# A two-block transformer on one core: in the compression of keys and values the weights become the operand that stays in the array

## The reference, cut to what matters

```python
def nsa_compress(t, gidx, pe, w1, w2):
    B = t.shape[0]
    blocks = t[:, gidx] + pe
    flat = blocks.reshape(B, gidx.shape[0], NSA_CMP_LEN * HEAD_DIM)
    return jax.nn.silu(flat @ w1) @ w2

    # in hybrid_layer
    nc = (S - NSA_CMP_LEN) // NSA_CMP_STRIDE + 1          # 15
    ...
    k_cmp = nsa_compress(kc, gidx, cmp_pe[0], cmp_w1[0], cmp_w2[0])
    v_cmp = nsa_compress(vc, gidx, cmp_pe[1], cmp_w1[1], cmp_w2[1])
```

## Time and profile before

| | us |
|---|---|
| median of three runs | 1888.17 (1887.89 to 1890.16) |
| the profiled execution, its own time | 1886.72 |
| its span, first to last instruction | 1884.9 |
| PE busy in the span | 1852.9 (98%) |
| PEld busy | 1761.4 (93%) |
| DVE busy | 1219.6 (65%) |
| ACT busy | 961.7 (51%) |

### The profile page before, as it was taken

The page is one execution under the profiler, slowest core; times in us unless marked ns, Lnnn a source line. Parts: engine busy times, 40 slices in busy tenths (PEclk is TensorE's granted clock), DMA queues, the critical chain, the costliest instruction groups (busy, mean ns, idle before and its releaser), DMA issues.

```text
span 1884.9 us, 34776 instructions
## 1 busy us (share of the span) xinstructions
PE 1852.9 (98%) x14842; PEld 1761.4 (93%) x14842; DVE 1219.6 (65%) x1876; ACT 961.7 (51%) x1475; POOL 67.7 (4%) x32
## 2 busy tenths in 40 slices
PE   7999999999999999999999999999999999999999
PEld 7999998989999999999989989999988989988989
DVE  6775576655766567756676557665674578763676
ACT  6544567255644354435672556444553565653562
POOL 0000011400000000000114000000000000000000
PEclk9999999999999999999999999999999999999999
DMA  8555543233555655555432335555546435546332
GB/s 328 188 183 186 174 143 112 90 119 110 186 189 182 209 182 189 183 187 170 156 112 90 107 118 172 186 190 180 168 149 200 143 111 170 163 147 216 122 110 94
DMA packets 84457, 302.34 MB, mean 160 GB/s; under 512 B 9168, under 2 KB 11728, under 8 KB 84176
## 3 DMA queue, kind: packets, MB, share of 16 engines
q1 hardware_dynamic: 84304, 300.13, 48.2%
HBM read 299.04 MB, written 1.05 MB: 159 GB/s over the span
## 4 chain that ended last, share of the span: by engine, by line
PE 91%; DVE 5%; ACT 3%; issue 1%; DMA 0%; SPq 0%; DVEq 0%; ACTq 0%
PE bank L395 22%; PE bank L398 22%; PE bank L399 22%; PE bank L698 3%; DVE w_lo L1560 2%; PE bank L927 1%; PE bank L417 1%; PE bank L416 1%; PE bank L413 1%; PE bank L460 1%; PE bank L1012 1%; PE bank L464 1%; PE bank L465 1%; PE bank L1063 1%; PE bank L628 1%; PE bank L632 1%
## 5 line engine op out<-in xcount | busy, mean ns | idle before, releaser
L1560 DVE TENSOR_TENSOR w_lo<-ring,w_hi 128x1024 fp32r<-128x1024 f32 x544 | 659.1, 1245 | 113.0 <-ACT w_hi L1130 112.3
L1130 ACT ACTIVATE w_hi<-ring 128x1024 fp32r<-128x1024 f32 x544 | 563.6, 1053 | 284.5 <-PE bank L395 225.2
L395 PE MATMUL bank<-xs,w_hi 128*128 128x256 f32 x2448 | 693.9, 283 | 0.0
L399 PE MATMUL bank<-xs,w_lo 128*128 128x256 f32 x2448 | 684.5, 280 | 0.0
L398 PE MATMUL bank<-xs,w_hi 128*128 128x256 f32 x2448 | 684.5, 280 | 0.0
L395 PEld LDWEIGHTS bank<-xs,w_hi 128*128 128x128 f32 x2448 | 463.5, 189 | 4.9 <-issue 3.8
L398 PEld LDWEIGHTS bank<-xs,w_hi 128*128 128x128 f32 x2448 | 462.2, 189 | 3.1 <-issue 2.9
L399 PEld LDWEIGHTS bank<-xs,w_lo 128*128 128x128 f32 x2448 | 462.1, 189 | 0.0
L398 PE MATMUL bank<-a,w_hi 128*128 128x256 f32 x704 | 199.0, 283 | 0.0
L395 PE MATMUL bank<-a,w_hi 128*128 128x256 f32 x704 | 198.7, 282 | 0.0
L399 PE MATMUL bank<-a,w_lo 128*128 128x256 f32 x704 | 197.7, 281 | 0.0
(11 more groups left out here) (393 smaller groups left out, 3112.4 us busy)
## 6 DMA issues: line engine op xcount, KB each, us to landing
ring<-in_w SPq DMA_DIRECT2D x560, 512.0 KB, 3.4
arena<-in_mem SPq DMA_DIRECT2D x2, 1024.0 KB, 12.7
const<-in_const SPq DMA_DIRECT2D x1, 1395.0 KB, 15.5
h<-in_x SPq DMA_DIRECT2D x1, 768.0 KB, 6.5
out<-h SPq DMA_DIRECT2D x3, 256.0 KB, 2.5
dec_par<-in_dec SPq DMA_DIRECT2D x1, 615.0 KB, 18.9
h<-in_x SPq DMA_DIRECT2D x1, 256.0 KB, 3.8
out<-h SPq DMA_DIRECT2D x2, 128.0 KB, 2.0
```

The source lines that it names most:

```text
L395: last = nc.tensor.matmul(o, wh, hi(x, k0 + k), start=k == 0, stop=False, skip_group_check=True)
L399: last = nc.tensor.matmul(o, wl, hi(x, k0 + k), start=False, stop=k == nk - 1, skip_group_check=True)
L1130: nc.scalar.activation(w_hi[:, s * UNIT:(s + 1) * UNIT], ring[:, u % RU, :], AF.Copy).then_inc(sems("w_hi"), 1)
L1560: nc.vector.tensor_tensor(w_lo[:, r * UNIT:(r + 1) * UNIT], ring[:, r, :], w_hi[:, s * UNIT:(s + 1) * UNIT].bitcast(F32), ALU.subtract).th ...
```

## The change

The operands trade places. For each of the 32 positions there are two matmuls in place of one: each loads a 128x128 half of the weights' block, and the 30 columns of `flat` pass. The sum lands in bank 5 in 128 partitions (the inner features) by 2 x 30 columns. So it already stands as the next product needs it: the two transposes, ACT's copy of them, the wait for each and the buffer `hid_t` go, and ACT's silu now reads 128x60 in place of 30x256. The table of shared semaphores has a line less of names and is otherwise dealt anew; its rows aren't shown.

```diff
-        flat, hid, hid_t = take(32, 2 * NCMP), take(2, 2 * NCMP), take(T)
+        flat, hid = take(32, 2 * NCMP), take(2, 2 * NCMP)
...
                 for l in range(32):
                     blk, first = w.block(2)
-                    last = nc.tensor.matmul(bank[5][0:2 * NCMP, 0:T], flat[:, l, :], blk, start=l == 0, stop=l == 31,
-                        skip_group_check=True)
-                    if first:
-                        last.then_inc(sems("unit_begun"), 1)
-                    elif l == 31:
+                    for ht in range(2):
+                        last = nc.tensor.matmul(bank[5][:, ht * 2 * NCMP:(ht + 1) * 2 * NCMP], blk[:, ht * P:(ht + 1) * P],
+                            flat[:, l, :], start=l == 0 and ht == 0, stop=l == 31, skip_group_check=True)
+                        if first and ht == 0:
+                            last.then_inc(sems("unit_begun"), 1)
+                    if l == 31:
                         last.then_inc(*pe.tell('hid_full'))
...
                 filler(2)
-                pe.e.wait_ge(*pe.need('hid_s', 1))
-                for ht in range(2):
-                    last = nc.tensor.transpose(bank[6][:, ht * 2 * NCMP:(ht + 1) * 2 * NCMP],
-                        hid_t[0:2 * NCMP, ht * P:(ht + 1) * P], ident[0:2 * NCMP, 0:2 * NCMP])
-                last.then_inc(*pe.tell('hid_turned'))
                 filler(2)
                 pe.e.wait_ge(*pe.need('hid_e', 1))
...
                 a.e.wait_ge(*a.need('hid_full', 1))
-                nc.scalar.activation(hid_t[0:2 * NCMP, :], bank[5][0:2 * NCMP, 0:T], AF.Silu).then_inc(*a.tell('hid_s'))
-                a.e.wait_ge(*a.need('hid_turned', 1))
-                nc.scalar.activation(hid, tiles(bank[6][:, 0:4 * NCMP], 2), AF.Copy).then_inc(*a.tell('hid_e'))
+                nc.scalar.activation(hid, tiles(bank[5][:, 0:4 * NCMP], 2), AF.Silu).then_inc(*a.tell('hid_e'))
```

More of the change, by code:

```diff
@@ L88 @@
               qs_full="g_full", rot_full="c_full", kv_full="o_half", fv_part="row_full", fv_full="gcol_full",
[L89 to L97, removed]
@@ L98 @@
-              q_sin="y", qr="gcol", flat="dt", xf="mixed", lf="k_out", z_r="qkn", gl_e="rr", fcol="kb",
-              kcn="kq", kc="kend", pc_d="lt", pcn="qkd", nm="xt_up", ob="x_up", up_out="r1", mgd="mix_lo")
+              gf_full="os_full", hid_full="f_full", gl_full="l_full", kc_full="vt_full", vc_full="brow_full",
+              fcol_full="kt_full", kcs_full="gram_full", krot_full="kq_full", cs_full="xy_full",
+              ct_full="y_full", o_part="xyt_full", up_full="vn_full", m_rstd="ff_e", q="ff_e", f_rstd="ff_e",
@@ new lines @@
+              few="m_sq", xo_hi="m_sq", behind="m_hi", p="m_hi", pt="v_sb", f_sq="v_sb", q_sq="ab", q_ln="zl",
+              q_rstd="b_e", masks="l_sb", v="y0", fv="a_sb", gf="o_out", gate_e="o_sq", ft="os_out",
+              z_out="os_rstd", hid_e="ys", kc_sq="l_sq", vc="gz_e", forget_hi="l_ln", kcs_ln="l_rstd",
+              kcs_rstd="dte", pc_e="eg", gl_s="yy", ptc="f_out", mg_hi="vn", fgain="x_lo", wab="g_r", mx="g_r",
+              half_bg="g_r", qk="ff", pn="ff", zs_in="m_ss", xo_lo="m_ss", wgf="m_ss", gg="m_lo", f_var="m_lo",
@@ L102 @@
+              f_ss="sp_sb", raw="sp_sb", qn="g_out", q_sin="y", qr="gcol", flat="dt", xf="mixed", lf="k_out",
+              z_r="qkn", gl_e="rr", fcol="kb", kcn="kq", kc="kend", pc_d="lt", pcn="qkd", nm="xt_up",
+              ob="x_up", up_out="r1", mgd="mix_lo")
 FFN_UNITS = 3 * KF
```

## The result

The changed kernel takes 1911.89 us (median of four runs, 1906.68 to 1913.84) against 1888.03 us (median of four runs of the kernel before, 1882.54 to 1890.16). The ratio is 1.0131 (95% interval 1.0113 to 1.015), so 1.3% slower. The profiled execution took 1911.89 us (1886.72 before), its span is 1910.1 us, and the mean granted clock is 0.986 (0.999 before). All four runs of the changed kernel show a mean granted clock of 0.985 or 0.986.

A forecast was written before the change was run, and what follows sets the result against it. TensorE's stream was taken to bound the kernel. Passes and transposes, 2 x (0.7 - 0.4) = +0.6 us, gave 1888.8 on the median's scale; clock falls of 24.0 made 1912.8, stated as 1912.5, range 1908 to 1918 (over all cases 1887.5 to 1917).

The forecast's parts named there:

- The bound: Whole kernel: TensorE's stream sets the time, PE busy for 98% of the span and holding 91% of the chain.
- The passes at full clock: Compression stage: 128 passes set by their loads, 0.113 us each, 14.6 us in place of 13.9, +0.7 us a layer.
- The 53 ns of line 990: Rival: loads run side by side at 0.053 us a step, stage 6.8 us, 1873 us; chance 0.04 with other gains over 0.2%.
- The transposes: Behind the compression's matmuls: without the two transposes, the following line starts earlier, -0.4 us a layer.
- ACT and the DMAs: Shorter silu, dropped copy and slightly slower filling of the weights' ring: off the path, buying nothing.
- The clock falls in both stages: Compression stage, both layers: clock drops to 0.50 after 3.7 us, costing 12.0 us a layer, 24.0 in all; chance 0.58.
- The stalls behind it: Behind the keys' normalisation: 2.1 us stalls stay; whether a short 0.50 stretch follows may differ, 1.7 us each.
- the sum (24.6 us): Whole kernel: +0.6 us from passes and transposes in both layers, plus 24.0 us from the clock's falls.

The follow-up runs named there:

- Experiment 1: The changed kernel with the 30 columns sent four times in each pass (120 columns), same loads: 1885.89 us, ratio 1.0001 to the kernel before.
- Experiment 2: The changed kernel with the 30 columns sent twice in each pass (60 columns), same loads: 1886.53 us, ratio 1.0001 to the kernel before.
- experiment 3: The change made in the first of the two layers only, the second left as in the kernel before: 1898.16 us, ratio 1.0074.
- experiment 4: The kernel before, with two of the four filler pieces behind the keys' rotation put ahead of it to cover TensorE's stall: 1884.61 us, ratio 0.9991.
- experiment 6: The old orientation, with positions sent to four 32-column groups of the array and a stacked identity adding and turning the sums: 1866.87 us, ratio 0.9909.
- experiment 7: The old orientation in four column groups, with two filler pieces also put ahead of the keys' rotation: 1860.54 us, ratio 0.9871 to the kernel before.
- experiment 5: The changed kernel with two filler pieces put ahead of the keys' rotation to cover TensorE's stall: 1904.81 us, ratio 1.0101 to the kernel before.

## Why the prediction was right, point by point

- *The bound.* Right. TensorE's stream is the path in both kernels, and each microsecond it loses is one of the kernel's.
- *The passes at full clock.* The step of 0.113 us, taken from line 958's 15 columns, holds for 30, 60 and 120: 0.112 in the changed kernel's first loads and in experiments 1 and 2. The stage at full clock is 14.2 to 14.3 us, where I had 14.6. The 53 ns of line 990 played no part.
- *The transposes.* From the stage's first load to the end of the span, the kernel before takes 1884.9 - 1445.7 = 439.2 us, 437.5 without the 1.7 us of its one stretch at 0.50. Experiment 1, at full clock throughout, takes 1884.1 - 1446.8 = 437.3. So the change without the clock is worth -0.1 us a layer, where I had +0.3. The difference is too small to be timed: the executions of either kernel scatter by some microseconds. Experiment 1 passes 120 columns and not 30, so it stands in for the change at full clock, and no run shows that one for a whole stage.
- *ACT and the DMAs.* Nothing came of them, as forecast: in both stages, and in the filler behind the first, PE is busy for all of the windows shown, so it waited for neither a split nor a unit.
- *The clock falls in both stages.* Right, and experiments 1 and 2 show the cause: more passing columns beside the same loads undo it. Ahead of the result no row had shown it: I gave it 0.58, on a single fall behind idle time. The fall came 3.3 us after the stage's start (1446.4 to 1449.7) in the first layer and 3.8 (1729.2 to 1733.0) in the second; I had 3.7. The stages last 24.3 and 23.8 us, where I had 14.6 + 10.7 = 25.3. Behind them 2.5 us (1471.0 to 1473.5) and 3.5 us (1753.3 to 1756.8) at half clock cost 1.3 and 1.8; I had 1.3 each.
- *The stalls behind it.* Left open, and it went to the worse side: a short stretch at 0.50 in both layers, 1.7 us more than before. (The stall's 2.1 us are 1.83 us of idle time and a short pair of matmuls; the forecast doesn't use the length.) It makes up for the stages, which were 1.0 and 1.5 us shorter than forecast. So the sum (24.6 us) came out closer to the 25.2 us between the profiled executions than its terms deserve; that part is luck.

The Trainium skill's page "TensorE: Matmul & The Clock Gate" says in Part 1 that the clock gate follows how busy the engine has been. The trace agrees only if "busy" leaves out the loads: with PE and PEld both busy for the whole of 23.8 us the clock stood at 0.50, and with the same loads and more columns at 1.00. The 25 ns for a matmul of up to 64 columns, of its section "Back-to-back issue gap", don't hold for this form: 112 ns at full clock, with a 128x128 float load ahead of each pass.

## What to carry to other kernels

Before swapping operands to let fewer columns pass, count the loads and read a row with the same load: where the load sets the step, fewer columns win nothing, and they can bring the clock down, which doubled every step here (0.11 to 0.21 us) until some microseconds after the full streams had returned. Read the clock row beside the busy row, since a TensorE that is 100% busy at 0.50 looks healthy in the latter. If the operand that stays has few columns, fill the rest of the array with other such operands rather than turn the product over: here that was worth 0.9%, and the swap cost 1.3%.

## What the runs showed of the hardware that I had not expected

- More work is faster: the same 128 loads a layer with 60 or 120 columns each take 14.2 to 14.3 us, with 30 columns 24.3 and 23.8.
- Plain-float matmuls in four column groups of 32 overlap almost fully: 64 passes of 256 columns in 3.59 us against 13.93.
- Short falls of 3.4 us stand also behind stretches in which TensorE is busy all the time. They have their place: in the profiles of experiments 3, 4, 6 and 7 in the first layer, and of 4, 5 and 7 in the second, they follow the same piece of the program, and in those of both kernels and of experiments 1 and 2 none stands there. In experiment 4, 128 rounded columns pass in each step of 0.11 us up to 1423.5 (256 pass in such a step elsewhere), then eight passes of 18 columns take 1.3 us (lines 431 and 433), and the clock falls at 1425.0. Experiment 2's stage has plain loads with 60 columns each for 14 us and held the clock; what tells the two apart these runs leave open.
- The scatter of the kernel before (1880.55 to 1893.34 us over 25 executions) goes in part with the granted clock: the three slowest, 1892.81 to 1893.34, are the three at 0.996, and the eight at 1.000 take 1880.55 to 1886.45. So some 6 us of scatter are left at full clock, which weren't traced.
